# A fused two-layer decoder step: z, k and v projections as seven-product pairs among the recurrence's matmuls, and sixteen gate tiles in the paired gate stage

## The chip, the core and the metric

The kernel runs on one core of a Trainium2 chip. The time is the device time of one execution in microseconds; the median of three runs is taken. The engines are named as in the profile: PE is TensorE's matmuls (PEld its weight loads), DVE is VectorE, ACT is ScalarE, POOL is GpSimd, SP is the queue of SyncE, which issues most weight transfers.

## The reference

Two layers (DEPTH = 2), 256 prompt tokens and 8 sample tokens side by side, so T = 264 columns; the model width is 2048 (16 blocks of 128), all in float32. Cut to what matters here:

```
h = x @ w_in                         # 2048 -> 11,952 columns
r, k, v, w_lo, a_lo, z = mixer A     # token shift: f + (prev - f) * mu
q, kc, vc, ks, vs, kw, vw, gl, z_b = mixer B
g_a, g_b = merge gates
o_A = rwkv scan(r, w, k, v, ...) * silu(z)
o_B = attention(q, k.., v..) * silu(z_b)
m = sigmoid(g_a) * (o_A @ w_up_a) + sigmoid(g_b) * (o_B @ w_up_b)
x = LayerNorm(ALPHA * x + m @ w_out)
```

## The kernel before

Everything is kept transposed: a tile is 128 output columns by 264 tokens, and x (XT) lies as 16 blocks of 128 by 264. A projection tile is made in one of two ways.

- Plain: sixteen matmuls of 264 columns into one PSUM bank, with 1 MB of weights in one of the two halves of WT. ACT copies the bank out when the tile is done (`take_out`). This needs nothing else of DVE and nothing of POOL.
- Paired: two tiles at once by a Strassen-like scheme of seven products (PRODUCTS = 7), each of eight matmuls of 132 columns, where plain tiles would take eight such blocks. Its price is in sums: of weights (OS1 to OS4, each 128 x 1024 elements, kept in TOEP), of x (MT or OT, once a stage), and of results. In the dense stages POOL makes OS1 and OS3 (`main_sums`, L647 and L650) and DVE makes OS2 and OS4 (L1886, L1891); ACT and DVE put the results together (c, d, u, om on ACT; f11, v, y, fin on DVE; for tiles with a token shift then mixa and mixb on DVE).

A layer goes through these stages in order, on every engine by a fixed program order:

1. `start`: two plain tiles (lo and the first kv).
2. `main_pairs`: 20 pairs back to back: v, k, r, z and eight kv tiles. Weights alternate between two sets of four blocks (MW).
3. The recurrence, four quads (hq 0 to 3). In each, PE makes a few small matmuls at a place and waits for DVE and ACT; while they work, PE runs matmuls of plain tiles ("fills") that `project` lets through up to a count written out for each place in BEHIND: low 16 (more in hq 0), bon 4, a1 11, tok 7, then y1 z1 ... y5 z5 one or two each, then r, u, s of four chunks one each. 18 plain tiles, 288 matmuls of 264 columns, are spread so in a layer, what is left at the place `mixers`.
4. The mixing stage: the sample tokens' state update on DVE (L2122 to L2140), GroupNorm, compression, attention. PE again runs plain tiles by the counts of BEHIND_MIX (vec 101, out0 46, ...); 26 tiles, of which 49 matmuls are left for the last place, `gates`.
5. `gate_pair` x4 (ga 8 to 15), `up_pair` x8, `out_pair` x8, LayerNorm.

The DVE's work in a quad begins with th (ACT) and runs lw (L1993), scan, kb, kf, kp, rk, at, rt, bt, kt (L2023); PE's a1 matmuls (L1093) wait for kt. Then g4 from PSUM (L2041), x0, x1, x2 (L2055), lm1 (L2057), and in each level one `lm` (L2063, two operands in SBUF) and one z (L2075, one of them in PSUM). PE's y1 waits for lm1.

POOL stands almost idle in the recurrence: it issues transfers at the end of each quad, and after the last:

```
                dma(TOEP[:, :, :], toep, d_toep)
                for hq in range(NQUAD):
                    po.wait_ge(*step("rw_v", L * NQUAD + hq, f"s{NCH - 1}"))
...
                dma(shift_t[L], SHO[:, :, :], st_shift)
                dma(kv_t[L], H[:, KV0:KV0 + 12, :], st_kv)
...
                po.wait_ge(st_wkv, (L + 1) * NPAIR * 16)
                halves = [slice(h * C // 2, (h + 1) * C // 2) for h in range(2)]
                for h, i in enumerate(halves):
                    dma(S4[:, i, :], states[L, :, i, :], d_state[h])
```

TOEP, the 2 MB bias table, is loaded at the start of the recurrence; the states (S4) are what the state update on DVE waits for.

The first gate pair takes its weights into the room of the queries (H) and of KNVC. Its loads wait for `zb_v out` (L2327), the last use of both; then POOL makes OS3 (L737) and OS1 (L739), DVE OS2 (L2343), while PE runs the fills left at `gates`.

## Time and profile before

| what | us or share |
|---|---|
| median of three runs | 2151.26 (2146.5 to 2156.7) |
| profiled execution, first to last instruction | 2147.6 |
| PE busy | 2111.1 (98%) |
| DVE busy | 1085.1 (51%) |
| ACT busy | 411.9 (19%) |
| POOL busy | 505.7 (24%) |
| granted TensorE clock, mean | 0.995 |

The profiled execution has no time of its own in the list beyond the span from its first to its last instruction. A float32 matmul of the program appears as two instructions in the profile: "x16" of L839 is one product of eight matmuls, "x32" of L791 one plain tile of sixteen. The bracket at the end of a timeline row is the idle time of the engine before it and what ended it. In the chain of waits the duration of a piece is the time that it adds to the chain; in the timeline it includes the end of the last matmul, so the chain is the one to price matmuls by.

### The profile page before, as it was taken

The page shows a single profiled execution, that of the slowest core. Times are in us where ns is not written, and L with a number is a line of the kernel's source. Part 1 is how long each engine was busy: PE and PEld are TensorE (multiplying, and loading weights), DVE is VectorE, ACT ScalarE, POOL GpSimd, SP SyncE. Part 2 cuts the span into 40 slices and gives each one's busy share as a digit, 9 for nine tenths or more (in the row PEclk, how much of TensorE's full clock was granted, in tenths as well). Part 3 has the DMA queues.
Part 4 walks back from the last instruction along what each step waited for, and adds up shares of the span by engine and source line. Part 5 has one row for each costly group of instructions (what it writes and reads, how often), then busy time and mean ns, then how long its engine had stood idle before and what let it go on. Part 6 is the DMA issues. An engine that isn't in the chain of part 4 may idle for free.

```text
span 2147.6 us, 48884 instructions
## 1 busy us (share of the span) xinstructions
PE 2111.1 (98%) x21468; PEld 1863.6 (87%) x21468; DVE 1085.1 (51%) x1884; ACT 411.9 (19%) x1169; POOL 505.7 (24%) x377
## 2 busy tenths in 40 slices
PE   9999999999999999999999999999999999999997
PEld 8999977777887779999999999777777877899996
DVE  4554344443726524773666442545557165247745
ACT  1111111222103411110211111222221143111002
POOL 3433300002011123333233333000020112134331
PEclk9999999999999999999999999999999999999998
DMA  8545333335543365554455454232264434655551
GB/s 299 175 160 173 117 133 101 101 101 220 198 138 119 114 220 177 164 178 160 133 182 166 166 166 139 83 101 101 101 243 165 133 104 144 218 169 164 173 169 66
DMA packets 88981, 329.51 MB, mean 153 GB/s; under 512 B 11905, under 2 KB 11921, under 8 KB 86465
## 3 DMA queue, kind: packets, MB, share of 16 engines
q1 hardware_dynamic: 74592, 268.60, 37.3%
q0 software_dynamic: 11872, 53.59, 7.1%
q10 hardware_dynamic: 2304, 4.20, 0.6%
q8 instruction: 169, 2.77, 0.5%
q14 instruction: 44, 0.35, 0.1%
HBM read 315.91 MB, written 18.82 MB: 156 GB/s over the span
## 4 chain that ended last, share of the span: by engine, by line
PE 96%; DVE 3%; DMA 1%; issue 0%; ACT 0%; SPq 0%; DVEq 0%
PE PB L791 30%; PE PB L839 3%; PE PB L870 3%; PE PB L866 3%; PE PB L861 3%; PE PB L854 3%; PE PB L844 3%; PE PB L850 3%; PE PB L1274 3%; PE PB L771 1%; PE PB L926 1%; PE PB L1008 1%; PE PB L991 1%; PE PB L993 1%; PE PB L986 1%; PE PB L982 1%
## 5 line engine op out<-in xcount | busy, mean ns | idle before, releaser
L791 PE MATMUL PB<-XT,WT 128*128 128x264 f32 (+1 forms) x2816 | 692.3, 395 | 0.3 <-DMA WT<-in_w_all 0.2
L791 PEld LDWEIGHTS PB<-XT,WT 128*128 128x128 f32 (+1 forms) x2816 | 509.4, 189 | 101.1 <-issue 15.2
L1480 ACT ACTIVATE VT<-PB 128x132 f32<-128x132 f32 (+2 forms) x280 | 79.1, 291 | 578.9 <-PE PB L854 130.6
L1480 ACT ACTIVATE ARENA<-PB 128x128 f32<-128x128 f32 (+7 forms) x187 | 76.3, 429 | 262.1 <-PE PB L1173 65.7
L626 POOL DMA_DIRECT2D out<-in_c_win x16 | 8.1, 506 | 456.2 <-DVE ARENA L2094 456.2
L626 POOL DMA_DIRECT2D ARENA<-in_c_sel x64 | 40.0, 625 | 234.4 <-issue 234.4
L647 POOL TENSOR_TENSOR TOEP<-WT 128x1024 f32<-128x1024 f32 x20 | 47.2, 2358 | 170.5 <-PE PB L854 160.9
L647 POOL TENSOR_TENSOR TOEP<-H 128x1024 f32<-128x1024 f32 x20 | 48.2, 2410 | 143.7 <-PE PB L854 136.5
L850 PE MATMUL PB<-ARENA,TOEP 128*128 128x132 f32 x640 | 78.5, 276 | 0.0
L854 PE MATMUL PB<-ARENA,TOEP 128*128 128x132 f32 x640 | 78.5, 276 | 0.0
L861 PE MATMUL PB<-ARENA,TOEP 128*128 128x132 f32 x640 | 78.5, 276 | 0.0
L870 PE MATMUL PB<-XT,TOEP 128*128 128x132 f32 x640 | 78.5, 276 | 0.0
L850 PEld LDWEIGHTS PB<-ARENA,TOEP 128*128 128x128 f32 x640 | 75.1, 190 | 0.0
L854 PEld LDWEIGHTS PB<-ARENA,TOEP 128*128 128x128 f32 x640 | 75.1, 190 | 0.0
L861 PEld LDWEIGHTS PB<-ARENA,TOEP 128*128 128x128 f32 x640 | 75.1, 190 | 0.0
L870 PEld LDWEIGHTS PB<-XT,TOEP 128*128 128x128 f32 x640 | 75.1, 190 | 0.0
L1274 PE MATMUL PB<-ARENA 128*128 128x288 f32 x256 | 62.7, 406 | 0.0
L1931 DVE TENSOR_TENSOR VT<-PB,VT 128x264 f32<-128x264 f32 x40 | 17.3, 432 | 86.1 <-PE PB L870 86.1
L1274 PEld LDWEIGHTS PB<-ARENA 128*128 128x128 f32 x256 | 48.6, 190 | 13.3
L2430 DVE TENSOR_TENSOR VT<-VT 128x132 f32<-128x132 f32 x32 | 47.4, 1519 | 24.1 <-ACT VT L1480 24.1
L1692 ACT ACTIVATE ARENA<-ARENA 128x128 f32<-128x128 f32 (+1 forms) x128 | 56.2, 443 | 16.2 <-DVE ARENA L2258 16.2
L1513 ACT ACTIVATE H<-PB 128x264 f32<-128x264 f32 x48 | 18.7, 389 | 208.0 <-PE PB L791 207.8
(475 smaller groups left out, 4203.5 us busy)
## 6 DMA issues: line engine op xcount, KB each, us to landing
WT<-in_w_all SPq DMA_DIRECT2D x340, 512.0 KB, 4.4
H<-in_w_all SPq DMA_DIRECT2D x120, 512.0 KB, 4.6
KNVC<-in_w_all SPq DMA_DIRECT2D x40, 512.0 KB, 3.8
out<-in_c_win POOLq DMA_DIRECT2D x16, 512.0 KB, 5.2
ARENA<-in_c_cmp POOLq DMA_DIRECT2D x64, 128.0 KB, 4.4
ARENA<-in_c_sel POOLq DMA_DIRECT2D x64, 128.0 KB, 4.1
TOEP<-in_toep POOLq DMA_DIRECT2D x2, 2048.0 KB, 8.7
ARENA<-in_states POOLq DMA_DIRECT2D x4, 1024.0 KB, 11.4
```

The lines of the kernel that those rows point to most:

```text
L647: mark("ms_p", it, add(OS1, w[2], w[3], ALU.add), "s1")
L791: ins = mm(PB[rows, bank, 0:T], WT[:, s, k, 0:rows.stop - rows.start], x, start=start, stop=stop)
L839: mm(a, w[0][:, k, :], XT[:, k, t0], start=k == 0, stop=k == BLK - 1)
L844: ins = mm(b, w[1][:, k, :], XT[:, BLK + k, t0], start=False, stop=k == BLK - 1, skip_group_check=True)
L850: mm(c, OS3[:, k, :], MT[:, 2, k, :], start=k == 0, stop=k == BLK - 1)
L854: ins = mm(d, OS1[:, k, :], MT[:, 0, k, :], start=False, stop=k == BLK - 1, skip_group_check=True)
L861: ins = mm(a, OS2[:, k, :], MT[:, 1, k, :], start=False, stop=k == BLK - 1, skip_group_check=True)
L866: ins = mm(c, w[3][:, k, :], MT[:, 3, k, :], start=False, stop=k == BLK - 1, skip_group_check=True)
L870: ins = mm(d, OS4[:, k, :], XT[:, BLK + k, t1], start=False, stop=k == BLK - 1, skip_group_check=True)
L1274: ins = mm(PB[:, 3 * (s // 8) + gp, 0:CMP_N], W1D[:, s, :], x, start=s % 8 == 0, stop=s % 8 == 7)
L1480: return act(out, in_, ACT.Copy)
L1692: ins = act(x, x, ACT.Exp, bias=NM[u % 3][:, t, i:i + 1], accum_out=RSM[u % 3][:, t, i:i + 1])
```

## The change

- MAIN keeps v, k and r: 12 pairs instead of 20. NORM_PAIR moves from 10 to 8.
- The z tiles and all twelve kv tiles become FILL: ten pairs, whose 56 matmuls of 132 columns each are the fills of the recurrence (560 units). All counts of BEHIND and BEHIND_MIX are in units of 132 columns, so twice the old ones.
- All four weight sums of a fill pair (s3, s1, s2, s4) are POOL's (`fill_sums`); there is one set of weight blocks (FW = WT) and one of each sum, so each waits for the product that reads it to be done in the pair before. Result sums (f11, v, y, fin) and, for z, the token shift stand in DVE's program between the steps of the recurrence (`mix` at low0 to low3, a1a to a1c, toka, tokb and so on), the copies in ACT's.
- The sums of x (MT) lie in the room of q and zb, so q and zb tiles are no longer made in the recurrence: the plain tiles of the mixing stage are q, zb and gb 0 to 7, 24 instead of 26, of which 17 matmuls of 264 columns are left at `gates`.
- OS1 to OS4 lie in TOEP, so the bias table is loaded after the last fill pair, ahead of the stores of shift and kv and of the loads of the states on POOL's queue.
- gb 8 to 15 and ga 0 to 7 go to the gate stage: GATES is 12 instead of 4.
- gl takes the place of the first kv tile at the start, with all 128 columns; before, its matmuls had 64 columns.

```
-TILES = ([("lo", LO)] + [("kv", KV0 + i) for i in range(8, 12)] + [("gl", GL)] + [("q", Q0 + i) for i in range(8)]
-         + [("zb", ZB0 + i) for i in range(8)] + [("gb", i) for i in range(16)] + [("ga", i) for i in range(8)])
+TILES = ([("lo", LO), ("gl", GL)] + [("q", Q0 + i) for i in range(8)] + [("zb", ZB0 + i) for i in range(8)]
+         + [("gb", i) for i in range(8)])
 N_TILES = len(TILES)
-EARLY = 20
-MAIN = ([("v", V0 + i) for i in range(8)] + [("k", K0 + i) for i in range(8)] + [("r", R0 + i) for i in range(8)]
-        + [("z", Z0 + i) for i in range(8)] + [("kv", KV0 + i) for i in range(8)])
+MAIN = [("v", V0 + i) for i in range(8)] + [("k", K0 + i) for i in range(8)] + [("r", R0 + i) for i in range(8)]
 MAINS = len(MAIN) // 2
-K_PAIR, R_PAIR, KV_PAIR = 4, 8, 16
-NORM_PAIR = 10
+K_PAIR, R_PAIR = 4, 8
+NORM_PAIR = 8
 LAST_ODD, EVENS = MAINS - 1 - MAINS % 2, (MAINS + 1) // 2
-PAIRED = [("ga", i) for i in range(8, 16)] + [("up", i // 2 + i % 2 * 8) for i in range(16)] + [("out", i) for i in range(16)]
-GATES, UPS, PAIRS = 4, 8, 8
+FILL = [("z", Z0 + i) for i in range(8)] + [("kv", KV0 + i) for i in range(12)]
+FILLS, Z_FILLS = len(FILL) // 2, 4
+GATED = [("gb", i) for i in range(8, 16)] + [("ga", i) for i in range(16)]
+PAIRED = GATED + [("up", i // 2 + i % 2 * 8) for i in range(16)] + [("out", i) for i in range(16)]
+GATES, UPS, PAIRS = len(GATED) // 2, 8, 8
...
-BEHIND = {"low": 16, "bon": 4, "a1": 11, "tok": 7}
+
+FILL_AT = 2 * UNITS_OF_TILE
+FILL_END = FILL_AT + FILLS * UNITS_OF_PAIR
+UNITS_OF_LAYER = FILL_END + (N_TILES - 2) * UNITS_OF_TILE
+
+
+def tile_at(i):
+    return i * UNITS_OF_TILE if i < 2 else FILL_END + (i - 2) * UNITS_OF_TILE
+
+
+def fill_at(i):
+    return FILL_AT + i * UNITS_OF_PAIR
+
+
+def schedule(tiles, **behind):
+
+    table = [(tile_at(i) + UNITS_OF_TILE, "tile", i) for i in tiles]
+    for i in range(FILLS):
+        for name, units in behind.items():
+            if name != "mix" or i < Z_FILLS:
+                table.append((min(fill_at(i) + units, FILL_END), name, i))
+    return sorted(table, key=lambda row: row[0])
+
+
+ACT_TABLE = schedule(range(N_TILES), c=17, d=33, u=41, om=59)
+DVE_TABLE = schedule([0], f11=18, v=34, y=42, fin=57, mix=61)
+
+
+BEHIND = {"low0": 8, "low1": 8, "low2": 8, "low3": 8, "bon": 8, "a1a": 8, "a1b": 8, "a1c": 6, "toka": 7, "tokb": 7}
 for level in range(1, LEVELS + 1):
-    BEHIND.update({f"y{level}": 1 if level < LEVELS else 2, f"z{level}": 2 if level < LEVELS else 4})
+    BEHIND.update({f"y{level}": 2 if level < LEVELS else 4, f"z{level}": 4 if level < LEVELS else 8})
 for chunk in range(NCH):
-    BEHIND.update({f"r{chunk}": 1, f"u{chunk}": 1, f"s{chunk}": chunk // (NCH - 1)})
-
-
-BEHIND_MIX = {"v0": 4, "v1": 4, "v2": 4, "v3": 4, "vec": 101, "mu": 5, "mu2": 3, "sq": 0, "var": 10, "gbc": 5, "bc2": 5,
-              "h0": 12, "out0": 46, "h1": 12, "out1": 10}
-BEHIND_MIX.update({"cb": 12, "cbt": 3, "sc1": 4})
+    BEHIND.update({f"r{chunk}": 2, f"u{chunk}": 2, f"s{chunk}": 2 * (chunk // (NCH - 1))})
+
+
+BEHIND_MIX = {"v0": 8, "v1": 8, "v2": 8, "v3": 8, "vec": 202, "mu": 10, "mu2": 6, "sq": 0, "var": 20, "gbc": 10, "bc2": 10,
+              "h0": 24, "out0": 92, "h1": 24, "out1": 20}
+BEHIND_MIX.update({"cb": 24, "cbt": 6, "sc1": 8})
...
+        FQ, FQU = take(P, 2 * T), KNVC[:, 8 * T:8 * T + HALF]
...
-        MT = OT
+        MW = [[*(block_of(keys_values, b * BLK * P) for b in range(3)), block_of(ARENA, at_up - 4 * BLK * HALF)], PW[1]]
+        FW = PW[1]
+        MT = [flat(H[:, t:t + 4, :]).rearrange("p (k n) -> p k n", n=HALF) for t in (Q0, Q0 + 4, ZB0, ZB0 + 4)]
...
+            def load_fills(L):
+
+                last = L * MAINS + LAST_ODD
+                sp.wait_ge(*step("ms_p", last, "s3"))
+                load_fill(L, 0, 2)
+                sp.wait_ge(*step("mp_t", last, "st1"))
+                sp.wait_ge(*step("ms_v", last, "s2"))
+                load_fill(L, 0, 0)
+                sp.wait_ge(*step("ms_v", last, "s4"))
+                load_fill(L, 0, 1)
+                sp.wait_ge(*step("mp_t", last, "st4p"))
+                load_fill(L, 0, 3)
+                for i in range(1, FILLS):
+                    old = L * FILLS + i - 1
+                    sp.wait_ge(*step("fs_p", old, "s1"))
+                    load_fill(L, i, 2)
+                    sp.wait_ge(*step("fp_t", old, "st1"))
+                    sp.wait_ge(*step("fs_p", old, "s2"))
+                    load_fill(L, i, 0)
+                    sp.wait_ge(*step("fs_p", old, "s4"))
+                    load_fill(L, i, 1)
+                    sp.wait_ge(*step("fp_t", old, "st4p"))
+                    load_fill(L, i, 3)
...
+            def fill_sums(L, i, name):
+                it = L * FILLS + i
+                if i:
+                    po.wait_ge(*step("fp_t", it - 1, {"s3": "st2", "s1": "st2", "s2": "st3", "s4": "st4"}[name]))
+                else:
+                    po.wait_ge(*step("mp_t", (L + 1) * MAINS - 1, {"s3": "st2", "s1": "st2", "s2": "st3", "s4": "st4"}[name]))
+                    po.wait_ge(*step("ms_v", (L + 1) * MAINS - 1, "s4"))
+                if name == "s3":
+                    fill_loaded(po, L, i, 0)
+                    fill_loaded(po, L, i, 2)
+                    mark("fs_p", it, add(OS3, FW[0], FW[2], ALU.subtract), "s3")
+                elif name == "s1":
+                    if i:
+                        po.wait_ge(*step("fs_p", it - 1, "s2"))
+                    fill_loaded(po, L, i, 3)
+                    mark("fs_p", it, add(OS1, FW[2], FW[3], ALU.add), "s1")
+                elif name == "s2":
+                    if i:
+                        po.wait_ge(*step("fs_p", it - 1, "s4"))
+                    po.wait_ge(*step("fs_p", it, "s1"))
+                    mark("fs_p", it, add(OS2, OS1, FW[0], ALU.subtract), "s2")
+                else:
+                    fill_loaded(po, L, i, 1)
+                    po.wait_ge(*step("fs_p", it, "s2"))
+                    mark("fs_p", it, add(OS4, FW[1], OS2, ALU.subtract), "s4")
+
+            summed = [0]
+
+            def sums_until(L, units):
+
+                while summed[0] < 4 * FILLS * (L + 1):
+                    i, k = divmod(summed[0] - 4 * FILLS * L, 4)
+                    if fill_at(i) - (24, 8, 8, 0)[k] > units:
+                        break
+                    fill_sums(L, i, ("s3", "s1", "s2", "s4")[k])
+                    summed[0] += 1
...
-                po.wait_ge(*step("mp_a", L * MAINS + MAINS - 1, "om"))
+                po.wait_ge(*step("mm_v", L * MAINS + MAINS - 1, "mixb"))
                 nc.gpsimd.memset(flat(VT)[:, :], 0.0)
                 mark("yl_p", L, nc.gpsimd.memset(YL[3][:, :, :], 0.0), "zero")
-                dma(TOEP[:, :, :], toep, d_toep)
                 for hq in range(NQUAD):
+                    sums_until(L, UPTO[L, hq, f"s{NCH - 1}"] - L * UNITS_OF_LAYER)
                     po.wait_ge(*step("rw_v", L * NQUAD + hq, f"s{NCH - 1}"))
                     for w in range(2):
                         dma(win_old[L, 2 * hq + w], c_win[L, 2 * hq + w], st_win)
                         dma(wkv_prompt[L, 2 * hq + w], ST[:, NCH % 2, w, :], st_wkv)
-                all_projected(po, L, "q", 7)
-                po.wait_ge(*step("mm_v", L * MAINS + KV_PAIR - 1, "mixb"))
+                sums_until(L, UNITS_OF_LAYER)
+                po.wait_ge(*step("fp_t", (L + 1) * FILLS - 1, "st4"))
+                dma(TOEP[:, :, :], toep, d_toep)
+                po.wait_ge(*step("fp_a", (L + 1) * FILLS - 1, "om"))
+                po.wait_ge(*step("fm_v", L * FILLS + Z_FILLS - 1, "mixb"))
+                all_projected(po, L, "gl", 0)
                 dma(shift_t[L], SHO[:, :, :], st_shift)
                 dma(kv_t[L], H[:, KV0:KV0 + 12, :], st_kv)
...
+            def fill_unit(L, i, unit):
+
+                it = L * FILLS + i
+                t0, t1 = slice(0, HALF), slice(HALF, T)
+                first, second = PB[:, 6, :], PB[:, 7, :]
+                a, b, d, c = first[:, t0], first[:, t1], second[:, t0], second[:, t1]
+                product, k = divmod(unit, BLK)
+                last = k == BLK - 1
+                if product == 0:
+                    if k == 0:
+                        if i:
+                            pe.wait_ge(*step("fp_a", it - 1, "u"))
+                        else:
+                            pe.wait_ge(tile_out[0], L * N_TILES // 2 + 1)
+                        fill_loaded(pe, L, i, 0)
+                    mm(a, FW[0][:, k, :], XT[:, k, t0], start=k == 0, stop=last)
+                elif product == 1:
+                    if k == 0:
+                        fill_loaded(pe, L, i, 1)
+                    ins = mm(b, FW[1][:, k, :], XT[:, BLK + k, t0], start=False, stop=last, skip_group_check=True)
+                    if last:
+                        mark("fp_t", it, ins, "st1")
+                elif product == 2:
+                    if k == 0:
+                        pe.wait_ge(*step("fs_p", it, "s3"))
+                        if i:
+                            pe.wait_ge(*step("fp_v", it - 1, "fin"))
+                        else:
+                            pe.wait_ge(tile_out[1], L * N_TILES // 2 + 1)
+                    mm(c, OS3[:, k, :], MT[2][:, k, :], start=k == 0, stop=last)
+                elif product == 3:
+                    if k == 0:
+                        pe.wait_ge(*step("fs_p", it, "s1"))
+                    ins = mm(d, OS1[:, k, :], MT[0][:, k, :], start=False, stop=last, skip_group_check=True)
+                    if last:
+                        mark("fp_t", it, ins, "st2")
...
+            def fill_sum(L, i, name):
+
+                it = L * FILLS + i
+                first, second = PB[:, 6, :], PB[:, 7, :]
+                if name == "f11":
+                    ve.wait_ge(*step("fp_a", it, "c"))
+                    mark("fp_v", it, tt(FQ[:, 0:HALF], FQ[:, 0:HALF], first[:, HALF:T], ALU.add), "f11")
+                elif name == "v":
+                    ve.wait_ge(*step("fp_a", it, "d"))
+                    mark("fp_v", it, tt(FQ[:, T + HALF:2 * T], FQ[:, T + HALF:2 * T], second[:, HALF:T], ALU.add), "v")
+                elif name == "y":
+                    ve.wait_ge(*step("fp_a", it, "u"))
+                    ve.wait_ge(*step("fp_v", it, "v"))
+                    mark("fp_v", it, tt(FQ[:, T + HALF:2 * T], FQ[:, T + HALF:2 * T], FQU[:, :], ALU.add), "y")
+                elif name == "fin":
+                    ve.wait_ge(*step("fp_t", it, "st4"))
+                    mark("fp_v", it, tt(FQ[:, HALF:HALF + T].rearrange("p (a n) -> p a n", n=HALF),
+                                        second[:, 0:T].rearrange("p (a n) -> p a n", n=HALF),
+                                        spread(FQU[:, :].unsqueeze(1), P, 2, HALF), ALU.add), "fin")
+                else:
+                    ve.wait_ge(*step("fp_a", it, "om"))
+                    for j in range(2):
+                        t = FILL[2 * i + j][1]
+                        x, dest = FQ[:, j * T:j * T + T], H[:, t, :]
+                        mu = PT[:, L, MU + t:MU + t + 1]
+                        cp(SHO[:, t, :], x[:, SEQ - 1:T])
+                        stt(dest[:, 1:SEQ], x[:, 0:SEQ - 1], mu, dest[:, 1:SEQ], ALU.mult, ALU.add)
+                        mark("fm_v", it, stt(dest[:, SEQ:T], SHT[:, L, t, :], mu, dest[:, SEQ:T], ALU.mult, ALU.add), "mix" + "ab"[j])
...
+                main_mix(L, MAINS - 1)
...
+                    mix(L, hq, "low0")
                     for w in range(2):
                         ins = nc.vector.tensor_tensor_scan(CS[:, w, :], SCAN, LW[:, w, 0:SEQ], 0.0, ALU.mult, ALU.add)
                     v("cum", ins)
+                    mix(L, hq, "low1")
                     wait("gate")
                     v("kb", tt(BB[:, :, :], kn, AV[:, 0], ALU.mult))
                     for w in range(2):
@@ -2005,10 +2256,12 @@
                     v("kf", ins)
                     wait("kf")
                     v("kp", tt(KP[:, :, :], kk, KF[:, :, :], ALU.mult))
+                    mix(L, hq, "low2")
                     wait("kp")
                     for w in range(2):
                         ins = stt(RK[:, w, :], rr[:, w, :], par(PRK, w), KP[:, w, :], ALU.mult, ALU.mult)
                     v("rk", ins)
+                    mix(L, hq, "low3")
```

## Rows read from the trace of the kernel before

**Rows 1.** The page: busy time, share of the span, instructions.
```profile
span 2147.6 us, 48884 instructions
PE 2111.1 (98%) x21468; PEld 1863.6 (87%) x21468; DVE 1085.1 (51%) x1884; ACT 411.9 (19%) x1169; POOL 505.7 (24%) x377
```

**Rows 2.** The chain of waits in order of time: start, us, what.
```profile
34.09 1.80 PE PB L839 x16
...
304.15 3.01 PE PB L791 x14
...
508.28 7.32 PE PB L791 x32
```

**Rows 3.** The page: costliest groups and transfers (KB each, us to landing).
```profile
L1931 DVE TENSOR_TENSOR VT<-PB,VT 128x264 f32<-128x264 f32 x40 | 17.3, 432 | 86.1 <-PE PB L870 86.1
...
TOEP<-in_toep POOLq DMA_DIRECT2D x2, 2048.0 KB, 8.7
```

**Rows 4.** Timeline, POOL and DVE together, start of layer 1.
```profile
1085.73 2.36 POOL L647 TENSOR_TENSOR TOEP<-WT 128x1024 f32<-128x1024 f32 x1 [27.24 <-PE PB L854]
...
1086.21 0.42 DVE L1850 TENSOR_SCALAR ARENA<-PB 128x264 f32<-128x264 f32 x1
1086.67 1.71 DVE L1854 SCALAR_TENSOR_TENSOR ARENA<-ARENA 128x264 f32<-128x264 f32 x1
1088.05 2.55 POOL L650 TENSOR_TENSOR TOEP<-WT 128x1024 f32<-128x1024 f32 x1
1088.41 2.47 DVE L1855 TENSOR_TENSOR ARENA<-ARENA 128x264 f32<-128x264 f32 x1
```

**Rows 5.** Timeline of one quad of layer 0 (hq 1), PE first, then DVE.
```profile
397.06 7.39 PE L791 MATMUL PB<-XT,WT 128*128 128x264 f32 x32
...
407.05 1.98 PE L1093 MATMUL PB<-ARENA 64*64 64x128 f32 x64
...
398.96 0.44 DVE L1993 TENSOR_SCALAR ARENA<-ARENA 128x528 f32<-128x528 f32 x1 [3.04 <-ACT ARENA L1572]
...
405.73 0.69 DVE L2023 TENSOR_TENSOR ARENA<-ARENA 128x512 f32<-128x512 f32 x1
...
418.09 0.68 DVE L2057 TENSOR_TENSOR ARENA<-ARENA,CM 128x512 f32<-128x512 f32 x1
421.04 0.69 DVE L2063 TENSOR_TENSOR ARENA<-ARENA,CM 128x512 f32<-128x512 f32 x1 [2.27 <-PE PB L1126]
423.22 0.69 DVE L2075 TENSOR_TENSOR ARENA<-ARENA,PB 128x512 f32<-128x512 f32 x1 [1.49 <-PE PB L1159]
```

**Rows 6.** Timeline around the state update of layer 0.
```profile
517.66 1.05 POOL L626 DMA_DIRECT2D ARENA<-in_states  x2 [5.14 <-DMA out<-ARENA]
...
527.90 2.29 DVE L2122 TENSOR_TENSOR ARENA<-ARENA 128x2048 f32<-128x2048 f32 x1 [9.03 <-DMA ARENA<-in_states]
...
569.70 0.19 DVE L2140 COPY ARENA<-ARENA 64x64 f32<-64x64 f32 x1
...
571.00 2.91 PE L1235 MATMUL PB<-H,CM 128*128 128x264 f32 x12 [0.41 <-DVE H L2142]
```

**Rows 7.** Transfer rate in 40 equal slices of the stretch 505 to 530 us.
```profile
GB/s 0 0 0 0 0 46 157 118 275 347 426 865 282 3 501 387 91 453 482 371 426 446 385 373 389 420 419 439 393 380 459 380 446 426 419 406 419 419 377 387
```

**Rows 8.** Timeline around the start of the gate stage, layer 0.
```profile
782.58 21.97 PE L791 MATMUL PB<-XT,WT 128*128 128x264 f32 x98
...
786.07 2.36 DVE L2327 SCALAR_TENSOR_TENSOR H<-H,ARENA 128x2112 f32<-128x2112 f32 x1
...
791.19 0.43 SPq L505 DMA_DIRECT2D H<-in_w_all  x1
...
802.16 2.35 POOL L739 TENSOR_TENSOR TOEP<-KNVC 128x1024 f32<-128x1024 f32 x1 [0.23 <-DMA KNVC<-in_w_all]
```

**Rows 9.** Timeline, the step from the main pairs to the recurrence.
```profile
276.53 1.80 DVE L1964 TENSOR_TENSOR KNVC<-KNVC,PB 128x1584 f32<-128x1584 f32 x1 [1.34 <-PE PB L1051]
```

**Rows 10.** Stretches: us, busy of PE, PEld, DVE, ACT, POOL, PEclk, DMA share, GB/s.
```profile
1745.00:1750.00 5.00, 3.18 (x11) 2.69 (x11) 4.93 (x7) 4.19 (x17) 0.00 (x0) 0.70 0.00 0
```

296 lines of the change are left out of this document (186 added, 110 removed).

## The prediction

> **What bounds the kernel.** I read the page first: PE is busy 2111 of 2147.6 us [rows 1], so time is saved only by less PE work, and any wait put on PE is paid in full. The chain of waits prices that work: a product of eight 132-column matmuls adds 1.80 us (0.225 us a unit), a plain tile of sixteen 264-column ones 7.32 us [rows 2]. Then I read the timelines of the seams, because a full PE can hide that the chains beside it have no slack. Two have none. In a quad DVE works from 398.96 to 406.42 and a1 starts at 407.05, directly behind PE's fills; lm1 ends at 418.77 and its y copy and lm come at 421.04, one level after the other every 4 us [rows 5]. In the state update the states are asked for at 517.66, DVE starts on them at 527.90 and ends at 569.9, and PE, whose 101 fills of the place vec cover this, goes on at 571.0 having waited 0.41 us for DVE [rows 6].
>
> **PE work.** Main and gate pairs together stay 24. Plain tiles go from 44 to 24 in a layer (20 x 7.32 = 146.4 us less) and ten fill pairs come (10 x 7 x 1.80 = 126.0 more): 20.4 us saved. From this about 1.0 goes back, since gl had matmuls of 64 columns: a piece of seven matmuls, three of them gl's, adds 3.01 us where 7 x 0.4575 = 3.20 is due [rows 2], 0.06 each, 16 of them. Net 19.4 us a layer.
>
> **Main to recurrence.** With r as the last pair, its copies and token shift stand ahead of kn on DVE, which now starts at 276.53, one idle PE gap before the low matmuls [rows 9]. Some six small DVE operations come first, of which the three fill groups of a shift cost 1 to 2 us; PE's eight fills hide part. I take +1.0 (0 to 2).
>
> **Result sums.** Each fill pair adds four DVE operations of up to 0.43 us [rows 3] and, for z, six more. Between levels DVE has gaps of 1.5 to 2.3 us [rows 5], which hold them; at low it has none, and about 40% of a pair falls there in each quad. Four quads, 0.4 to 0.6 us each: +2.0 (0 to 5).
>
> **Weight sums on POOL.** A fill pair needs four POOL operations of 2.36 us, 40 in a layer, 94 us in a recurrence of 228. The trace of before has no such operations in the recurrence, so I look where POOL and DVE work side by side [rows 4]. POOL runs two sums from 1085.73 to 1090.60. A DVE operation with its one large operand in PSUM takes 0.42 us beside the first. The next, of the same 264 columns but with two operands in SBUF, takes 1.71 and ends just behind POOL's, and the next one 2.47 and ends just behind POOL's second. So beside back-to-back POOL sums DVE completes one such operation for each POOL sum. The Trainium skill ("SBUF — State Buffer", section "SBUF: two separate sides") says why: the port pair that VectorE and GpSimd share is an exclusive lock held for a whole instruction. By that rule too, an operation with two SBUF inputs waits and one with a PSUM input does not; were the ports only shared in proportion, the two operations would take perhaps twice their time and the term below would be a few us. The trace agrees with the lock.
>
> In a quad some 27 DVE operations have two operands in SBUF (or are all in SBUF): 16 of the low part, x0, x2, lm1, four lm, four d. When do POOL's sums come? s1, s2 and s4 of pair j follow each other and wait for block 3, which is loaded after unit 56j - 8 and lands some 4 to 5 us later: a burst of 7.1 us. s3 comes alone, after unit 56j - 24. I count the units of the places (hq 1 begins at 156, 286 and 416 begin hq 2 and 3 in layer 0) against the times of rows 5.
> - A burst in low (j = 3: unit 160, 1 us after low began; it runs from about 5.8 to 12.9 us of the quad, over mix, rk, at, rt, bt, kt): DVE gets three or four locked operations through in 7.1 us instead of a dozen; kt is late by 5.5 us, 7 with the shift of pair 2 caught in it. PE's a1 waits that long. In hq 0, pair 0's last sums, s3 of pair 1 and its burst meet the same steps; 3 us of spare fills there, and I put 7.
> - A burst over x2 and lm1 (j = 4, 6): two boundaries of 2.36 us, less 0.4 of slack: 4 each.
> - A burst over levels or chunks (j = 2, 5, 7, 8, 9): one locked operation each 3 to 4 us with 1.5 us of slack behind it, so 0.5 each.
> - s3 in low (j = 6, 8): 2 each; elsewhere 1 together.
>
> This makes 14 + 8 + 2.5 + 5 = 29.5 us. Stalls shift the later bursts into places with more slack, and POOL gives way now and then, so I take +25 a layer. Nothing at all is lost if the sums fall beside PSUM operands only: that is the lower bound, 0. The upper one is 45, half of POOL's 94 us. This is the largest term and the least certain.
>
> **State update.** Its cover shrinks by what is left at `mixers`: 15 matmuls of 264 columns (6.9 us) become 14 of 132 (3.2 us) in layer 0, and 9 (4.1) become 2 (0.5) in layer 1; PE is done 3.6 us earlier and must wait for a DVE chain that is not earlier: +3.6 (PE's saved work is already in the 20.4). And the 2 MB bias table, hidden before, now stands in POOL's queue before the stores and the states. That stretch moves some 400 GB/s already without a gap [rows 7], so 2.1 MB more delay the states by 2.1 / 0.41 = 5.1 us; bounds 2 (some of it fits into the thin slices before 511 us) and 8.7, its own landing time [rows 3]. DVE starts on the states when they land, so all of it is paid. Together +8.7 (5.6 to 12.3).
>
> **Start of the gate stage.** Before, 49 fills (22 us) covered zb, the loads, and the two POOL sums; OS1 was ready at 804.5, 22.0 us after they began, with 5 us to spare [rows 8]. Now 17 fills, 7.8 us. zb is still done at 788.4, 5.9 us in; SP is free then instead of at 791.2, and 2 MB are to be loaded instead of 3. Loads need 5 us for the first two blocks, 8 for all; OS1 is then ready at 5.9 + 8 + 2.4 = 16.5 us, and product 3, which needs it, could start at 7.8 + 5.4 = 13.2. +3.5 (2 to 6). The eight gate pairs that follow are dense like the main ones.
>
> **The sum.** Per layer: -19.4 + 1.0 + 2.0 + 25 + 8.7 + 3.5 = +20.8; two layers +41.6. The span goes from 2147.6 to 2189; the profiled span is 3.7 below the median of the runs, which gives 2151.3 + 41.6 = **2193**.
>
> **Rivals.**
> 1. *POOL's sums cost nothing (the other side).* If DVE's locked operations and the sums miss each other, or the quads have slack that I don't see, the term of 25 is gone: -4.2 a layer, 2143. For it: PE's fills keep their counts at every place, and DVE idles half of the time [rows 1]. Against: rows 4, and a low part in which DVE has no idle time [rows 5]. It decides once the term is under 4 us a layer.
> 2. *The seams are covered as well.* If the bias table also finds room and the loads of the gate stage come early, all of 19.4 a layer is left: 2151 - 39 = 2112. Against: 0.41 us of slack [rows 6].
> 3. *The clock falls too.* When PE waited in 1745 to 1750 it was granted a mean of 0.70 of the clock, that is 1.2 GHz for part of the stretch instead of 2.4 [rows 10]. Waits of 7 us at a1 and 9 us behind vec would bring that about more often; a product then takes 3.6 us, and two or three us are lost at each of some ten long waits: +25 in all: 2218.
>
> **Chances.** The forecast as summed 0.50; rival 3 0.15; rival 1 0.20; rival 2 0.15. A difference under 0.5% (10.8 us) can't be told from none here: 2140.5 to 2162 is "same". Rival 1 lies on that edge, and a tenth of the forecast's spread reaches in. Faster 0.15 + 0.08 = 0.23; same 0.11 + 0.02 = 0.13; slower 0.64. The likeliest case alone spans 2160 to 2220 (term 12 to 38 a layer). The range of 8 in 10 reaches over rival 1 and into rival 3: 2125 to 2225.
>
> **What would show it.** Right: in the recurrence, the DVE rows of the low part, of x2, lm1 and lm with durations up to 2.4 us instead of 0.4 to 1.2, ending just behind rows of POOL; idle time of PE before a1 and y1, released by DVE; quads of 62 to 66 us instead of 57. The states landing 14 to 16 us after their issue, and 9 us idle before the matmuls of YS. OS1's sum ending behind the last plain tile. Wrong: quads of 57 us or less with POOL busy for 22 of them; a state update that starts no later after the last quad than before; main and gate pairs that take other than 12.6 us.

## The result and the profile after

The changed kernel takes 2242.5 us (median of 4 runs, 2239.6 to 2246.4) against 2149.8 of the kernel before on the same chip: ratio 1.0426, 95% interval 1.0406 to 1.0446. It is slower by 93 us, where 42 were forecast; 2242.5 lies above the range. The profiled run is the longest of the four (2246.4 us), so its stages below add up to 97 us, not 93.

The page of the changed kernel [rows 1]: span, then busy time, share, instructions.

```profile
span 2244.7 us, 51162 instructions
PE 2124.1 (95%) x22428; PEld 1937.0 (86%) x22428; DVE 1194.5 (53%) x1964; ACT 422.0 (19%) x1201; POOL 706.3 (31%) x457
```

PE is busy for 13 us more than before although some 39 us of its work were taken out, and the span is 97 us longer. I cut both traces into stages, at the first matmul of each (main pairs, the low matmuls of each quad, YS, the end of the mix, the gate pairs). Microseconds, layer 0 / layer 1:

| stage | before | after | difference | forecast a layer |
|---|---|---|---|---|
| start, to the first product | 21.3 | 25.5 | +4.1 once | 0 |
| main and gate pairs | 303.7 / 304.6 | 306.7 / 307.2 | +3.1 / +2.6 | together with the mix: -11.1 |
| last main pair to low | 5.3 / 5.3 | 6.1 / 6.1 | +0.8 / +0.8 | +1.0 |
| the four quads | 228.1 / 236.2 | 269.8 / 286.9 | +41.7 / +50.7 | +25.8 |
| state update | 62.9 / 60.6 | 71.3 / 65.3 | +8.3 / +4.7 | +5.1 |
| mix, up to the gate pairs | 233.4 / 237.7 | 226.6 / 224.8 | -6.8 / -12.9 | (above) |

In the last column the 19.4 us of saved PE work are split by where the units lie: 1.2 in the quads (the cheap matmuls of gl, which take 1.0 back, lay in the first of them), 3.6 in the state update, 14.6 in the mix. The quads carry 92 of the 97 us. The recurrences as two stretches each, first of the kernel before, then of the changed one; the columns are those of [rows 10]:

```profile
280.00:508.10 228.10, 223.08 (x4296) 170.66 (x4296) 108.07 (x248) 46.04 (x134) 6.42 (x12) 1.00 0.29 99
1337.80:1574.10 236.30, 230.71 (x4324) 174.79 (x4324) 117.30 (x260) 49.41 (x142) 6.42 (x12) 1.00 0.30 100
```

```profile
184.60:454.40 269.80, 241.41 (x4832) 218.33 (x4832) 167.57 (x310) 53.66 (x160) 105.08 (x52) 0.94 0.28 89
1289.20:1576.10 286.90, 252.01 (x4872) 225.55 (x4872) 166.48 (x323) 56.32 (x168) 106.68 (x52) 0.92 0.27 86
```

POOL went from 6 to 105 us, as it had to. DVE went from 225 to 334 us in the two together, for 125 more instructions: its old ones became longer. PE stands idle for 28 and 35 us instead of 5 and 6, and is busy for 18 and 21 us more, at a mean granted clock of 0.94 and 0.92 instead of 1.00. The timeline of the low part of a quad (layer 0, hq 1) shows where, DVE first, then POOL, then PE [rows 5 and 4 answer to these]:

```profile
261.70 0.70 DVE L2253 TENSOR_TENSOR ARENA<-KNVC,ARENA 128x528 f32<-128x528 f32 x1
...
264.19 2.31 DVE L2076 SCALAR_TENSOR_TENSOR H<-SHT,PT,H 128x8 f32<-128x8 f32 x1
...
266.89 2.30 DVE L2076 SCALAR_TENSOR_TENSOR H<-SHT,PT,H 128x8 f32<-128x8 f32 x1
269.11 2.97 DVE L2262 SCALAR_TENSOR_TENSOR ARENA<-H,PT,ARENA 128x264 f32<-128x264 f32 x2
...
264.02 2.45 POOL L739 TENSOR_TENSOR TOEP<-WT 128x1024 f32<-128x1024 f32 x1 [5.72 <-DMA WT<-in_w_all]
266.64 2.52 POOL L744 TENSOR_TENSOR TOEP<-TOEP,WT 128x1024 f32<-128x1024 f32 x1 [0.17 <-POOL TOEP L739]
269.33 2.46 POOL L748 TENSOR_TENSOR TOEP<-WT,TOEP 128x1024 f32<-128x1024 f32 x1 [0.17 <-POOL TOEP L744]
...
272.13 2.13 PE L1260 MATMUL PB<-ARENA,CM 128*128 128x264 f32 x4 [7.07 <-DVE ARENA L2262]
```

This is the forecast picture. A sum's 2.45 us end at 266.47 and DVE's operation, begun at 264.19, at 266.50; the next two pairs end together as well. The operation that is held has 8 columns, so it isn't its own work that takes the time. PE then waits 7.07 us for rk, a step earlier than the a1 of the forecast. The longest groups of waits on PE in the whole kernel (us in total, times, longest):

```profile
PE PB L1260 <- DVE ARENA L2262: 16.3, 3, 8.2
PE PB L884 <- DVE ARENA L2394: 14.8, 2, 9.4
PE PB L1319 <- DVE ARENA L2312: 11.2, 3, 6.9
PE PB L951 <- DVE ARENA L2058: 10.8, 7, 2.5
...
PE PB L1061 <- DMA H<-in_w_all: 4.8, 2, 2.4
```

The waits stand at rk (L1260), at YS in the state update (L884), at y1, the first level, which waits for lm1 (L1319) and at the fill pairs' own result sums (L951). The timeline ties the first to POOL's sums, and the third fits them; whether these make up the 92 us, and what the lower clock costs, only experiments can tell.

### The profile page after: what moved, and what is told of

It is laid out like the page before. It is cut to its first block, busy times and chain, and to the rows that moved or that the text cites. A ratio compares the mean times of both kernels' runs of the same rounds, so it can differ in the third digit from the quotient of the medians.

```text
span 2244.7 us, 51162 instructions
## 1 busy us (share of the span) xinstructions
PE 2124.1 (95%) x22428; PEld 1937.0 (86%) x22428; DVE 1194.5 (53%) x1964; ACT 422.0 (19%) x1201; POOL 706.3 (31%) x457
## 4 chain that ended last, share of the span: by engine, by line
PE 79%; DVE 14%; DMA 3%; issue 2%; ACT 1%; POOL 0%; SPq 0%; DVEq 0%; ACTq 0%; POOLq 0%
PE PB L900 10%; PE PB L1451 3%; PE PB L1079 2%; PE PB L1088 2%; PE PB L1061 2%; PE PB L1084 2%; PE PB L1027 2%; PE PB L1047 2%; PE PB L1074 2%; PE PB L1070 2%; PE PB L1064 2%; PE PB L1043 2%; PE PB L1038 2%; PE PB L1031 2%; PE PB L1016 2%; PE PB L1021 2%
## 5 line engine op out<-in xcount | busy, mean ns | idle before, releaser
L900 PE MATMUL PB<-XT,WT 128*128 128x264 f32 x1536 | 362.9, 390 | 2.7 <-DMA WT<-in_w_all 2.7
L900 PEld LDWEIGHTS PB<-XT,WT 128*128 128x128 f32 x1536 | 285.4, 190 | 60.5 <-issue 10.2
L1657 ACT ACTIVATE ARENA<-PB 128x128 f32<-128x128 f32 (+7 forms) x227 | 86.3, 403 | 283.6 <-PE PB L1350 59.8
L739 POOL TENSOR_TENSOR TOEP<-WT 128x1024 f32<-128x1024 f32 x20 | 53.8, 2691 | 151.1 <-DMA WT<-in_w_all 151.1
L868 POOL TENSOR_TENSOR TOEP<-WT 128x1024 f32<-128x1024 f32 x20 | 47.1, 2356 | 148.8 <-PE PB L1074 78.7
L734 POOL TENSOR_TENSOR TOEP<-WT 128x1024 f32<-128x1024 f32 x20 | 49.3, 2463 | 123.4 <-PE PB L937 103.0
L868 POOL TENSOR_TENSOR TOEP<-KNVC 128x1024 f32<-128x1024 f32 x18 | 42.4, 2354 | 143.7 <-PE PB L1074 80.1
L719 POOL TENSOR_TENSOR TOEP<-WT 128x1024 f32<-128x1024 f32 x12 | 28.3, 2358 | 107.6 <-PE PB L1031 90.4
L1319 PE MATMUL PB<-ARENA 64*64 64x32 f32 x1024 | 46.8, 226 | 13.5 <-DVE ARENA L2312 11.2
L1319 PEld LDWEIGHTS PB<-ARENA 64*64 64x64 f32 x1024 | 42.8, 144 | 18.1 <-DVE ARENA L2312 11.8
L951 PE MATMUL PB<-H,WT 128*128 128x132 f32 x320 | 47.5, 293 | 10.8 <-DVE ARENA L2058 10.8
L951 PEld LDWEIGHTS PB<-H,WT 128*128 128x128 f32 x320 | 40.6, 195 | 14.1 <-issue 12.4
L884 PE MATMUL PB<-CM,ARENA 128*128 128x128 f32 (+4 forms) x242 | 34.1, 275 | 18.4 <-DVE ARENA L2394 14.8
L944 PE MATMUL PB<-H,TOEP 128*128 128x132 f32 x320 | 48.5, 299 | 3.0 <-DVE ARENA L2055 3.0
```

Of the source, the lines that this page charges most:

```text
L719: mark("ms_p", it, add(OS1, w[2], w[3], ALU.add), "s1")
L734: mark("fs_p", it, add(OS3, FW[0], FW[2], ALU.subtract), "s3")
L739: mark("fs_p", it, add(OS1, FW[2], FW[3], ALU.add), "s1")
L868: mark("os_p", L * BOTH + g, add(OS1, w[2], w[3], ALU.add), "s1")
L900: ins = mm(PB[:, 6 + s, 0:T], WT[:, s, k, :], XT[:, k, :], start=k == 0, stop=k == KT - 1)
L944: ins = mm(a, OS2[:, k, :], MT[1][:, k, :], start=False, stop=last, skip_group_check=True)
```

## The experiments

Each run used one core, with the kernel before beside it on the same chip. e1 to e4 ran on one chip, e5 to e11 on a second, e12 on a third; the kernel before took 2148.3 to 2151.0 us on them, so a difference in us between runs of different chips is good to about 3 us. Ratios are to the kernel before, with their 95% interval; quads are the sum over a layer in one profiled run, layer 0 / layer 1. e3, whose edit touches nothing in the quads, moved them by -3.1 / +5.0: a single trace's quads scatter by that much, in layer 1 above all.

| run | us | ratio | quads |
|---|---|---|---|
| changed kernel | 2242.5 | 1.0426 (1.0406 to 1.0446) | 269.8 / 286.9 |
| e1, sums of 8 columns | 2181.7 | 1.0142 (1.0103 to 1.0181) | 235.0 / 255.9 |
| e2, sums that read nothing | 2183.2 | 1.0153 (1.0117 to 1.0189) | 235.3 / 257.1 |
| e3, states first | 2230.6 | 1.0373 (1.0325 to 1.0422) | 266.7 / 291.9 |
| e4, sums in quarters | 2205.9 | 1.0258 (1.0221 to 1.0296) | 247.4 / 269.9 |
| e5, PE kept busy | 2241.8 | 1.0431 (1.0407 to 1.0455) | 268.7 / 283.6 |
| e6, e1 and small results | 2170.1 | 1.0097 (1.0068 to 1.0126) | 235.2 / 247.5 |
| e7, before and 80 sums | 2228.6 | 1.0365 (1.0342 to 1.0388) | 264.9 / 271.8 |
| e8, eighths, states first | 2189.3 | 1.0178 (1.0155 to 1.0202) | 248.8 / 265.2 |
| e9, e7 reading nothing | 2165.0 | 1.0060 (1.0039 to 1.0081) | 231.4 / 241.4 |
| e10, before in halves | 2164.8 | 1.0057 (1.0030 to 1.0085) | 230.4 / 248.1 |
| e11, sums on DVE | 2208.3 | 1.0261 (1.0233 to 1.0290) | 250.3 / 279.6 |
| e12, e10 again | 2165.0 | 1.0064 (1.0042 to 1.0086) | 230.3 / 247.2 |

**e1: take the sums away.** The same cut in all four sums:

```diff
-                    mark("fs_p", it, add(OS3, FW[0], FW[2], ALU.subtract), "s3")
+                    mark("fs_p", it, add(OS3[:, 0, 0:8], FW[0][:, 0, 0:8], FW[2][:, 0, 0:8], ALU.subtract), "s3")
```

> The changed kernel with the four POOL weight sums of every fill pair cut to 8 of 1024 columns (the rest of each sum is left out, so z and kv come out of stale weights); all waits, loads, matmuls and result sums stay. Theory (the sums hold VectorE's operations with two SBUF inputs, and this is most of the 46 us a layer by which the quads grew): the quads go back to 56 to 60 us each, the half-clock stretches in the recurrence go with the waits, and the time falls from 2242 to 2145 to 2175. Rival (the quads grew for another reason, the result sums or the order of the fills): quads stay above 64 us and the time above 2215.

2181.7: 60.8 less than the changed kernel, 7 above what the theory gave. The quads of layer 0 fall to 235.0 (228.1 before), those of layer 1 stop at 255.9 (236.2). So the sums are the bulk, and something else remains that is worse in layer 1.

**e2: keep POOL busy, without reading.**

```diff
-                    mark("fs_p", it, add(OS3, FW[0], FW[2], ALU.subtract), "s3")
+                    mark("fs_p", it, blank(OS3), "s3")
...
+            def blank(out):
+                for part in (out, out[:, 0:4, :]):
+                    nc.gpsimd.memset(part, 0.0).then_inc(blanked, 1)
+                    blanks[0] += 1
+                    po.wait_ge(blanked, blanks[0])
+                return nc.gpsimd.memset(out, 0.0)
```

> The changed kernel with each of the four POOL weight sums of a fill pair replaced by three fills with zero of the same tile (whole, half, whole; each waits for the one before), so POOL is busy for a similar time and the sums are marked done as late, but no POOL operation of a fill pair reads SBUF; the sums are left out (z and kv come out of zero weights). Theory (what holds VectorE is a POOL operation that reads SBUF beside it): quads of 56 to 62 us, 2145 to 2185 in all. Rival A (VectorE is held by any POOL operation, since all write SBUF): as slow as the changed kernel, 2225 to 2250. Rival B (the sums are simply late for PE): as slow too, but with PE waiting for POOL and not for VectorE.

2183.2, the same as e1. Its two recurrences:

```profile
181.10:416.40 235.30, 228.16 (x4832) 206.96 (x4832) 124.93 (x310) 53.74 (x160) 102.91 (x131) 1.00 0.31 102
1251.20:1508.30 257.10, 242.70 (x4872) 216.80 (x4872) 134.44 (x323) 56.42 (x168) 102.69 (x131) 0.97 0.29 96
```

POOL is as busy as in the changed kernel (206 against 212 us), DVE falls from 334 to 259 us. At the same place of the same quad the operations with two inputs are short again, beside a POOL that fills from 251.26 on:

```profile
251.26 0.22 DVE L2086 SCALAR_TENSOR_TENSOR H<-SHT,PT,H 128x8 f32<-128x8 f32 x1
251.40 0.83 DVE L2084 COPY SHO<-ARENA 128x9 f32<-128x9 f32 x1
...
252.01 0.89 DVE L2272 SCALAR_TENSOR_TENSOR ARENA<-H,PT,ARENA 128x264 f32<-128x264 f32 x2
...
251.26 1.53 POOL L755 MEMSET TOEP<- 128x1024 f32 x2 [5.88 <-PE PB L933]
252.85 0.96 POOL L758 MEMSET TOEP<- 128x1024 f32 x1
```

What is still longer is a COPY of 9 columns, 0.83 us for 0.17, with the operation that overlaps it. Both rivals fall. Neither POOL being busy nor the late sums cost the time, but POOL reading SBUF beside DVE: 334 - 259 = 75 us of DVE held, of which 556.7 - 492.4 = 64 us show in the quads, 32 a layer.

**e3: the bias table behind the states.**

```diff
-                dma(TOEP[:, :, :], toep, d_toep)
                 po.wait_ge(*step("fp_a", (L + 1) * FILLS - 1, "om"))
...
                     dma(S4[:, i, :], states[L, :, i, :], d_state[h])
+                dma(TOEP[:, :, :], toep, d_toep)
```

> The changed kernel with one edit in POOL's queue: the load of the 2 MB bias table stands behind the loads of the old states instead of ahead of them. Nothing is left out. Theory (the states land late because the table moves first): the states land about 10 us after their issue instead of 18.4 and 14.4, the state update is some 4 to 8 us shorter in each layer, 2227 to 2237 in all. Rival (the transfers behind it are short of bandwidth anyway, or the table is now late for the attention): within 4 us of the changed kernel.

2230.6, 11.9 less, as the theory had it. The changed kernel's states are asked for at 464.34, DVE starts on them at 482.81, and PE waits 9.39 us [rows 6]:

```profile
464.34 1.05 POOL L698 DMA_DIRECT2D ARENA<-in_states  x2 [2.90 <-DMA out<-ARENA]
...
482.81 2.29 DVE L2376 TENSOR_TENSOR ARENA<-ARENA 128x2048 f32<-128x2048 f32 x1 [20.34 <-DMA ARENA<-in_states]
...
524.86 0.37 PE L884 MATMUL PB<-CM,ARENA 64*128 64x64 f32 x1 [9.39 <-DVE ARENA L2394]
```

In e3 they land after 9.96 us and PE goes on without a wait:

```profile
457.79 1.05 POOL L698 DMA_DIRECT2D ARENA<-in_states  x2 [2.46 <-DMA out<-ARENA]
...
467.75 2.29 DVE L2376 TENSOR_TENSOR ARENA<-ARENA 128x2048 f32<-128x2048 f32 x1 [11.67 <-DMA ARENA<-in_states]
...
511.06 0.27 PE L884 MATMUL PB<-CM,ARENA 64*128 64x64 f32 x1
```

The state update is 63.8 / 61.3 us, only 0.8 / 0.7 longer than before. The table cost 7.5 / 4.0. The thinner cover cost the 3.6 of the forecast and 0.8 / 0.7 more: none of the 3.6 us of PE work saved in this stage shows in its length. PE's waits there are now for weights, 2.9 / 3.2 us.

**e4: sums in quarters.**

```diff
+            def pieces(out, a, b, op):
+                for k in range(0, BLK, 2):
+                    ins = add(out[:, k:k + 2, :], a[:, k:k + 2, :], b[:, k:k + 2, :], op)
+                return ins
```

> The changed kernel with each POOL weight sum of a fill pair issued as four sums of 256 columns in place of one of 1024. Nothing is left out; POOL does the same work with three more fixed costs for each sum. Theory (VectorE is held for the whole length of one POOL instruction, and is let in between two): a held operation ends after 0.6 to 0.8 us instead of up to 2.4, quads of 60 to 66 us, 2180 to 2215 in all. Rival (the two share SBUF in proportion to their work, whatever the pieces): 2240 to 2255, since POOL is busy a little longer.

2205.9, 36.6 less, with POOL busy for 271 us of the recurrences instead of 212. Shorter POOL instructions hold DVE for less, as the theory had it; the rival had this slower. The same 8-column operation (L2076 of the changed kernel) took 0.69 us beside pieces of 0.80, and in e8 below 0.42 beside pieces of 0.54:

```profile
258.73 0.42 DVE L2081 SCALAR_TENSOR_TENSOR H<-SHT,PT,H 128x8 f32<-128x8 f32 x1
...
258.60 4.35 POOL L726 TENSOR_TENSOR TOEP<-WT 128x128 f32<-128x128 f32 x8 [5.75 <-DMA WT<-in_w_all]
```

**e5: PE kept busy in its waits.**

```diff
+            def idle_work(n, to):
+
+                for _ in range(n):
+                    mm(to, ident, XT[:, 0, 0:to.shape[-1]], start=True, stop=True)
...
                     project(L, hq, "low3")
+                    if hq == 1:
+                        wait(("rw_a", "th"),)
+                        idle_work(12, PB[:, 3, 264:512])
```

> The changed kernel with matmuls of 248 to 256 columns whose result nobody reads, put on TensorE ahead of its longest waits: 12 ahead of rk in the second quad, 4 (layer 0) or 7 (layer 1) ahead of g40 in the first quad, 3 or 12 ahead of x1 in the second, 17 or 9 ahead of y2 in the state update. Nothing is left out. They should fit into waits of 1.5 to 9.4 us that the profile of the changed kernel shows there. Theory (about 30 of the 93 us lost are TensorE running at 1.2 GHz after such waits): the stretches at half clock behind these places go (from 78 us in the two recurrences and 17 in the state updates to under 30 in all), and the time falls by 15 to 35 to 2207 to 2227. Rival (while TensorE runs at half clock it is VectorE that sets the pace, so the clock costs nothing): 2237 to 2250, with the stretches gone.

2241.8: nothing gained that the noise would show. Half clock in a stretch is twice what its PEclk lacks of 1.00: in the changed kernel 2 x (0.06 x 269.8 + 0.08 x 286.9) = 78 us. In e5 the first two quads of layer 1, where most of it was (0.89 and 0.85), read:

```profile
1286.94:1364.15 77.21, 68.77 (x1254) 61.12 (x1254) 48.42 (x89) 15.43 (x45) 30.84 (x14) 0.96 0.24 77
1364.15:1442.62 78.47, 70.59 (x1260) 62.78 (x1261) 48.51 (x87) 14.28 (x42) 29.25 (x16) 0.98 0.26 83
```

In all eight quads, worked out in the same way, 33 us are left of the 78. The quads of the profiled run are 1.1 / 3.3 us shorter, within their scatter. The added matmuls (50 in the quads, at most 23 us at 0.4575 each) may have outlasted some waits, so that a gain of a few us could be hidden; the 15 to 35 of the theory are not there. The reading that fits is that DVE, busy for 332 us of these quads as against 334, sets their length, and PE at half clock only shortens its own waits.

**e6: the result sums gone as well.** Beside e1's edits, from the second fill pair on:

```diff
-                    mark("fp_v", it, tt(FQ[:, 0:HALF], FQ[:, 0:HALF], first[:, HALF:T], ALU.add), "f11")
+                    mark("fp_v", it, tt(FQ[:, 0:8], FQ[:, 0:8], first[:, HALF:HALF + 8], ALU.add), "f11")
...
-                        stt(dest[:, 1:SEQ], x[:, 0:SEQ - 1], mu, dest[:, 1:SEQ], ALU.mult, ALU.add)
```

> As e1_small_sums, and besides VectorE's four result sums of every fill pair but the first cut to 8 columns and its 255-column token shift left out, so that both POOL's sums and VectorE's part of the fills are nearly gone (weight sums, result sums and token shift of z are left out). Theory (the result sums are what keeps e1_small_sums at 2182, the forecast had only 2 us a layer for them): the quads of layer 1 fall from 63.8, 69.2, 59.9, 63.0 to about 60 each, those of layer 0 by 1 each, 2160 to 2170 in all. Rival (TensorE itself takes longer for twice as many matmuls of half the columns between the chain's own): within 6 of e1_small_sums, 2176 to 2188.

2170.1, 11.6 less than e1, on the edge of the theory. Layer 0's quads stay (235.2), layer 1's fall from 255.9 to 247.5: the result sums cost nothing in layer 0 and 8.4 in layer 1. Of the 8.4, 6.1 lie in its second quad, first of e1, then of e6:

```profile
1317.00:1386.30 69.30, 63.33 (x1214) 56.59 (x1214) 34.65 (x87) 14.28 (x42) 5.73 (x16) 0.93 0.28 94
1313.50:1376.60 63.10, 58.73 (x1212) 52.37 (x1212) 31.39 (x83) 14.28 (x42) 4.88 (x16) 1.00 0.31 103
```

PE's busy time falls by 4.6 us and its idle time by 1.6 for the same matmuls, and the clock is back from 0.93 to 1.00. So more than half of the 8.4 is lower clock: PE waits 2.3 us for rk and 2.0 for lm1 in e1, and is then slow in a quad that it nearly fills. e6 is still 7.1 and 11.3 us a layer above the kernel before, with neither sums nor results; PE is busy for 6.4 / 6.9 us more there and idle for 0.7 / 4.3 more.

**e7: the kernel before with POOL's part alone.**

```diff
                 for hq in range(NQUAD):
+                    for name, n in (("low", 4), ("y1", 4), ("r2", 2)):
+                        po.wait_ge(*step("rw_t", L * NQUAD + hq, name))
+                        for _ in range(n):
+                            add(OS3, OS1, OS2, ALU.add).then_inc(extra, 1)
+                            extras[0] += 1
+                            po.wait_ge(extra, extras[0])
```

> The kernel before with POOL's part of the change alone: in every quad ten sums of 1024 columns that nobody reads (four behind the low matmuls, four behind the first level, two behind the third chunk; each waits for the one before), 40 in a layer. For their tiles the bias table is loaded behind the states instead of at the start of the recurrence. Nothing is left out. Theory (the sums alone hold VectorE, and TensorE waits and loses its clock): 2149 becomes 2195 to 2235. Rival (they cost only together with the changed fills, where TensorE needs them in time): 2149 to 2165.

2228.6: 80 sums that nobody waits for, with the bias table behind the states, cost 80 us; e9 parts the two. The place of low in layer 0, hq 1, DVE and POOL:

```profile
346.79 1.78 DVE L2002 TENSOR_SCALAR ARENA<-ARENA 128x528 f32<-128x528 f32 x1 [3.04 <-ACT ARENA L1581]
348.51 2.56 DVE L2004 TENSOR_SCALAR ARENA<-ARENA 128x528 f32<-128x528 f32 x1
...
351.00 5.51 DVE L2008 TENSOR_TENSOR_SCAN ARENA<-CM,ARENA 128x256 f32<-128x256 f32 x2
356.43 0.68 DVE L2011 TENSOR_TENSOR ARENA<-KNVC,ARENA 128x528 f32<-128x528 f32 x1
...
345.91 10.05 POOL L677 TENSOR_TENSOR TOEP<-TOEP 128x1024 f32<-128x1024 f32 x4
```

While POOL's four sums run (345.91 to 355.96) DVE gets four long operations through, one each; the next takes its 0.68 us.

**e9: the same, reading nothing.** The sum of e7 replaced by three fills with zero of the same tile.

> As e7_before_with_sums, with each of the 40 sums a layer replaced by three fills with zero of its tile (whole, half, whole), which keep POOL about as busy and read no SBUF. Nothing is left out. Theory (what VectorE is held by is a POOL operation that reads SBUF): back to the kernel before, 2145 to 2158. Rival (the later bias table, the waits in POOL's queue or POOL's writes made the difference): 2200 to 2230.

2165.0, 63.6 less than e7 and outside the theory's range by 7. The low part again:

```profile
342.61 0.44 DVE L2003 TENSOR_SCALAR ARENA<-ARENA 128x528 f32<-128x528 f32 x1 [3.04 <-ACT ARENA L1582]
342.98 0.82 DVE L2005 TENSOR_SCALAR ARENA<-ARENA 128x528 f32<-128x528 f32 x1
...
343.72 1.26 DVE L2009 TENSOR_TENSOR_SCAN ARENA<-CM,ARENA 128x256 f32<-128x256 f32 x2
...
341.70 10.92 POOL L678 MEMSET TOEP<- 128x1024 f32 x12
```

The scan, with two operands, is free again; one TENSOR_SCALAR still took 0.82 instead of 0.42, so a POOL that only writes holds DVE a little. Of the 14 us left, the quads have 8.5 and the state updates 9.1 (the later table stands in their transfers; PE waits 2.4 us for weights in that of layer 0); other stages give some back.

**e8: eighths, and the states first.** `pieces` with one block of 128 columns at a time, and e3's edit.

> The changed kernel with each POOL weight sum of a fill pair issued as eight sums of 128 columns, and with the bias table loaded behind the old states. Nothing is left out. Theory (the wait of VectorE is one POOL instruction long, and both gains add up): 12 less than e4_quarter_sums by the states and some 5 to 15 by the shorter pieces, 2178 to 2195. Rival (fixed costs of eight instructions lengthen POOL's bursts until the sums are late for TensorE): 2195 to 2215.

2189.3, in the theory's range. If the table gives the 12 us of e3 here too, the rest of the 16.6 us below e4, some 5, is the shorter pieces'. The rival has a part in it: POOL is now busy for 328 us of the recurrences, and PE waits 7.2 us in the whole kernel for the sums themselves. This is the best complete form of the change that was run, and still 1.8% slower than the kernel before (1.6 to 2.0).

**e11: the sums on DVE.** `fill_sums` moves to VectorE with the marks `fs_v`, e3's order kept:

```diff
-DVE_TABLE = schedule([0], f11=18, v=34, y=42, fin=57, mix=61)
+DVE_TABLE = schedule([0], s3=-20, s1=6, s2=7, s4=14, f11=18, v=34, y=42, fin=57, mix=61)
```

> As e3_states_first, with the four weight sums of every fill pair made by VectorE, at its own places for the fills, instead of by POOL, which then has no work in the recurrence. Nothing is left out. A sum of 1024 columns should take VectorE 1.2 us, 49 us a layer. Theory (no lock, but VectorE's chain sets the pace of the quads, and about half of the sums fall where it has no gap): 20 to 30 us a layer of it is paid against 33 for the lock, 2195 to 2230. Rival (its gaps hold them all): 2165 to 2185, less than e8_eighths_states_first.

2208.3, 22.3 less than e3, in the theory's range. DVE needs 1.22 us for a sum (half of POOL's 2.45); but e8's eighths on POOL are better by 19. DVE is busy for 338 us of the recurrences here and for 284 in e8.

**e10 and e12: PE's part alone.** Each matmul of the kernel before's plain tiles split in two; below is e12's form.

```diff
-                    ins = mm(PB[rows, bank, 0:T], WT[:, s, k, 0:rows.stop - rows.start], x, start=start, stop=stop)
+                    for h in (slice(0, HALF), slice(HALF, T)):
+                        ins = mm(PB[rows, bank, h], WT[:, s, k, 0:rows.stop - rows.start], x[:, h], start=start and h.start == 0, stop=stop,
+                                 skip_group_check=True)
```

> The kernel before with each 264-column matmul of its plain tiles between the chain's steps (all but the first two tiles of layer 0) issued as two matmuls of 132 columns with the same weights. Nothing is left out. It does to TensorE in the gaps what the fill pairs do: twice the instructions, half the columns. Theory (this is what is left of the longer quads once sums and results are gone, 7 us in layer 0 and 11 in layer 1): quads 1 to 3 us longer each, 2160 to 2185 in all. Rival (two halves take the time of one whole, 0.45 against 0.4575 us, and what is left comes from waits between the products of a fill pair): 2140 to 2155.

> As e10_before_in_halves, but the second half of a tile no longer opens its sum anew (only the first half does, as in the paired stages), so the plain tiles hold what they hold in the kernel before; there the second opening changed part of their values. Nothing is left out. Theory (the time comes from the number of matmuls): 2155 to 2170 as there, with quads of layer 0 up by about 0.6 us each; in layer 1 one quad had been 7 us longer, with TensorE at half clock for 10 us behind a wait of 1.25 us, and that need not recur: 2155 without it. Rival (the second opening cost the time): within 5 us of the kernel before.

2164.8 and 2165.0, inside both theories' ranges. In e10 the second half opened its sum anew, which changes part of the plain tiles' values; the time is the same. By the dense prices two halves are a little cheaper than one whole (0.450 against 0.4575 us); between the chain's own matmuls they aren't. In layer 0 the quads are 2.2 us longer in all, 0.2 to 1.0 each. In the mixing stage, where the same tiles are split, e12 shows no clear price (+2.6 / -1.7). In layer 1 one quad of four takes 66 us instead of 60, in both runs at the same place:

```profile
1470.30:1536.30 66.00, 63.06 (x1212) 56.63 (x1212) 29.52 (x66) 11.99 (x35) 2.08 (x5) 0.92 0.28 98
```

```profile
1510.48 0.65 PE PB L792 x4
...
1511.88 1.80 issue
1513.68 0.24 PE PB L1158 x2
...
1514.23 2.00 PE PB L792 x8
```

In the chain of waits PE issues nothing for 1.80 us, which no semaphore explains, and then runs at 1.2 GHz: eight records of fill matmuls add 2.00 us. In e10 the gap is 1.25 us; eight such records add 1.10 us ahead of it and 2.06 behind. The clock of 0.92 over 66 us is 10.6 us at half clock, which is 5.3 lost. Here DVE is far from the bound (29.5 of 66 us), and the clock does cost its time. Why PE issues nothing is open; the kernel before has such a gap of 0.8 us in the same quad, without a loss of clock.

## Why the prediction was wrong

The direction, POOL's hold on DVE and the places were right; the size of the quads was not. Forecast +25.8 a layer, measured +46.2 (mean of the two layers). By the runs it is made of:

| part, us a layer | forecast | measured | from |
|---|---|---|---|
| weight sums on POOL | +25 | +33 | quads of the changed kernel less e1: 34.9 / 31.0; e2 gives 32, e7 against e9 32 |
| result sums | +2.0 | +4 | e1 less e6: -0.2 / 8.4 |
| PE work in the quads | -1.2 | +9 | e6 less before: 7.1 / 11.3 |

**PE work: the step that failed.** "A product of eight 132-column matmuls adds 1.80 us (0.225 us a unit), a plain tile of sixteen 264-column ones 7.32 us": both prices are from dense stretches, and I used them for units that are handed out in ones, twos and eights between matmuls of 32 and 64 columns. There the saving isn't found: with sums and results gone, e6's quads are 7.1 / 11.3 us longer than before. The error, some 10 us a layer, is larger than that of the largest term (8 for the weight sums); with 2 for the result sums the quads make 41 of the some 50 us by which the forecast missed.

How the +9 divides is shown only in part. In layer 0, hq 1 to 3 are 2.6 us longer in e6 and 2.0 in e12, so there it is the halves; hq 0 is 4.4 longer in e6 and 0.2 in e12, and 1.9 of it is half clock (0.97 of 63.7 us). In layer 1 the sums agree (11.3 and 11.0), but not the quads: e6 has +2.0, +4.5, -0.1 and +4.9, e12 has +3.3, +0.5, +6.5 and +0.8. In both, waits or gaps of 1 to 2 us stand in the longer of these quads (in e6's last one of 2.0 us for a fill pair's own result), some with half clock behind them. Why they come where they do, no run has taken apart.

**Weight sums: right, undersized.** 33 against 25, inside my bounds of 0 and 45. One burst in the low part was priced at 5.5 to 7 us, and PE's wait there was 7.07. What I left out is that DVE is held again and again where it has no slack: 75 us of holding became 64 us of time, where I gave the levels and chunks 0.5 us for each burst. 0.8 us of quad for each of 80 sums, in the changed kernel and in e7 alike, would have been the better rule.

**Result sums.** +2.0 was taken, 0 to 5 given: 0 in layer 0, 8.4 in layer 1. The forecast made no difference between the layers. DVE has three operations more in each quad of layer 1 (vd, vg, vm), which may be why waits show there; more than half of their price was lower clock (e6).

**State update.** +5.1 net forecast, +6.5 measured: the table 5.8 for 5.1 (e3), and 0.8 for the thinner cover, whose forecast of +3.6 gives back just the 3.6 of PE work saved here, 0 net.

**Seam and gate start.** The seam's +1.0 is 0.8. For the start of the gate stage I gave +3.5 (its sum 5.9 + 8 + 2.4 is 16.3, not 16.5, which changes nothing): PE waits 2.4 us for block 0 of the first gate pair, not for OS1, and the pairs of main and gates together are 2.9 longer than before (in layer 0, 0.77 us of it is a wait for DVE in the first gate pair, and 1.65 its first product, which takes 3.45 us to the next one's start instead of 1.80): 5 a layer. With the mix, -7.0 a layer came of the -11.1; the other 2 us are not taken apart. It was the load that was late, a step earlier than I put it:

```profile
752.23 3.61 PE L1061 MATMUL PB<-XT,H 128*128 128x132 f32 x16 [2.44 <-DMA H<-in_w_all]
...
762.01 2.04 PE L1079 MATMUL PB<-ARENA,TOEP 128*128 128x132 f32 x16 [0.77 <-DVE VT L2655]
```

The start of the kernel was 4.1 us later; the other runs have it between 21.7 and 24.7, so this is scatter in the first loads more than a cost of the change, and I can't say how much.

**The rivals.** Rival 1 (the sums cost nothing) is refuted by e1, e2 and e7, rival 2 with it (and by the 11.9 us of e3). Rival 3 was right that the clock would fall (78 us at half clock in the quads), and its +25 isn't found: e5 took more than half of that away and the time stayed. The clock cost time where PE set the pace (e12's long quad, e1's second quad of layer 1), and none that shows where PE waited for DVE.

## What to carry to other kernels

Before work goes to POOL beside a chain on DVE, count POOL's instructions that read SBUF and DVE's that do: here each 2.45 us sum cost 0.8 us of the quads, in the changed kernel and alone (e7 less e9). If it must go there, issue it in short pieces (the quarters gave back 37 of 61 us). Price filler work on PE at the grain at which it will run, by such a row, and not by a dense stretch; and ask which engine bounds the stretch before a granted clock below 1.00 is counted as lost time. A better place for its sums would not have made the change win: with them cut away it stood at 2181.7, and if e3's 11.9 us for the states come off that as well, it is still some 20 us above the kernel before.

## What the runs showed of the hardware

- The hold lasts to the end of the POOL instruction, whatever DVE's operation has to do: 8 columns took 2.31 us beside a whole sum, 0.69 beside quarters, 0.42 beside eighths, and 0.22 beside fills that read nothing (e2).
- It is not confined to operations with two inputs in SBUF: TENSOR_SCALARs with one, 128x528, took 1.78 and 2.56 us in e7 for 0.43 and 0.42. The prediction argued with two inputs, though its count of 27 takes in those that are all in SBUF. The Trainium skill ("SBUF — State Buffer", section "Who interferes with whom") has this too: such operations can run in a mode that takes both port pairs. The trace agrees with that, and with its rule that a POOL operation which only writes leaves two-operand ones alone (the scan's 1.26 us in e9). The COPY of 0.83 us in e2 and the TENSOR_SCALAR of 0.82 in e9 have one input and stood beside fills that only write.
- PE lost clock behind a gap of 1.80 us in e12 and of 1.25 us in e10, in a quad in which it was otherwise busy for 63 of 66 us (e12); a long wait is not needed.
- 132-column matmuls in place of 264-column ones raise PE's weight loading in layer 0's quads from 170.7 to 203.4 us (e12) and its busy time from 223.1 to 225.0:

```profile
283.90:514.10 230.20, 225.03 (x4830) 203.39 (x4832) 107.97 (x248) 45.99 (x134) 6.42 (x12) 1.00 0.29 98
```
